# Input slabs of the mixer, and two down projections, as seven products of halves; pieces of the modulation moved

## What is computed

```python
def _swiglu(h, w1, w3, w2):
    return (jax.nn.silu(h @ w1) * (h @ w3)) @ w2

for l in range(2):                                   # D_MODEL 1024, D_FF 2816, IN_W 3584
    ml = _modulation(c, w_ada[l], b_ada[l])          # silu(c) @ w_ada + b, nine vectors of 1024
    mc = _modulation(c_ctx[None], w_ada[l], b_ada[l])
    lat = lat + 0.5 * ml[2] * _swiglu(_modulate(lat, g1, ml[0], ml[1]), *ffn1)
    cx = cx + 0.5 * mc[2] * _swiglu(_modulate(cx, g1, mc[0], mc[1]), *ffn1)
    # mixer: z = h @ w_in, cut into u, v, q, f_fw, f_bw, i, og; q, f and i drive a gated scan
    ...                                              # cx and lat += m[5] * mixer(...)
    lat = lat + 0.5 * ml[8] * _swiglu(_modulate(lat, g3, ml[6], ml[7]), *ffn2)
    ...                                              # the same for cx, in layer 0 alone
```

## Time and profile before

| | |
|---|---|
| median of 3 runs | 3027.91 us (3026.37 to 3031.58) |
| the profiled execution | 3027.08 us, of which the span is 3024.9 us |
| TensorE matmul busy | 2844.2 us, 94% of the span |
| VectorE, ScalarE, GpSimd busy | 1049.0, 555.6, 439.4 us |
| first block, from the trace | to about 2213 us |
| experts at the end | from about 2587 us, waiting for weights |

### The profile page before, as it was taken

The page is one execution under the profiler, slowest core; times in us unless marked ns, Lnnn a source line. Parts: engine busy times, 40 slices in busy tenths (PEclk is TensorE's granted clock), DMA queues, the critical chain, the costliest instruction groups (busy, mean ns, idle before and its releaser), DMA issues.

```text
span 3024.9 us, 39799 instructions
## 1 busy us (share of the span) xinstructions
PE 2844.2 (94%) x17362; PEld 2418.2 (80%) x17362; DVE 1049.0 (35%) x1988; ACT 555.6 (18%) x842; POOL 439.4 (15%) x424
## 2 busy tenths in 40 slices
PE   8999999999999998999999999999999999866666
PEld 6888888888888898889888888889988888533432
DVE  3764034431433348433013433523146412210111
ACT  2101222123211101010023206210012340200000
POOL 0000011200121177058001210028100000000000
PEclk9999999999999999999999999999999999988878
DMA  9775443344333565554544344364433228899998
GB/s 405 272 272 183 151 152 125 127 152 153 139 138 127 195 251 211 186 230 167 168 153 153 134 139 157 129 224 168 167 125 134 103 94 337 367 429 431 429 431 373
DMA packets 74144, 641.47 MB, mean 212 GB/s; under 512 B 8304, under 2 KB 9584, under 8 KB 21232
## 3 DMA queue, kind: packets, MB, share of 16 engines
q1 hardware_dynamic: 71376, 631.55, 55.1%
q10 hardware_dynamic: 2592, 7.33, 0.6%
HBM read 637.80 MB, written 1.05 MB: 211 GB/s over the span
## 4 chain that ended last, share of the span: by engine, by line
PE 82%; DMA 12%; DVE 3%; issue 1%; ACT 1%; POOL 0%; SPq 0%; DVEq 0%; ACTq 0%; POOLq 0%
PE ps L1254 29%; PE ps L1276 18%; DMA ring<-in_w_moe 12%; PE ps L1234 10%; PE ps L1451 7%; PE ps L1264 3%; PE ps L1287 3%; PE ps L1481 2%; PE ps L1055 2%; PE ps L1340 1%; DVE work L1919 1%; DVE work L1913 1%; PE ps L1458 1%; PE ps L1077 1%; DMA ring<-in_w_ada 1%
## 5 line engine op out<-in xcount | busy, mean ns | idle before, releaser
L1254 PE MATMUL ps<-ring 128*128 128x256 f32 x2560 | 560.7, 380 | 0.2 <-ACT ring L1668 0.2
L1254 PEld LDWEIGHTS ps<-ring 128*128 128x128 f32 x2560 | 485.1, 190 | 68.4 <-issue 2.0
L1276 PE MATMUL ps<-work,ring 128*128 128x256 f32 x2464 | 537.9, 379 | 2.0 <-DVE work L1913 2.0
L1276 PEld LDWEIGHTS ps<-work,ring 128*128 128x128 f32 x2464 | 466.1, 190 | 66.5 <-DVE work L1913 2.2
L1254 PE MATMUL ps<-h,ring 128*128 128x256 f32 x1600 | 350.9, 380 | 6.4 <-ACT h L1668 4.2
L1913 DVE TENSOR_TENSOR work<-work,ps 128x128 f32<-128x128 f32 (+3 forms) x414 | 151.2, 400 | 577.0 <-PE ps L1254 292.8
L1254 PEld LDWEIGHTS ps<-h,ring 128*128 128x128 f32 x1600 | 301.0, 190 | 51.7 <-issue 5.6
L2604 POOL TENSOR_TENSOR ring<-ring 128x512 f32<-128x512 f32 x174 | 240.7, 1412 | 367.2 <-DMA ring<-in_w 320.0
L2632 POOL TENSOR_TENSOR work<-work 128x128 f32<-128x128 f32 x168 | 100.2, 635 | 1193.9 <-ACT work L1694 1193.9
L1234 PE MATMUL ps<-work,ring 128*128 128x128 f32 x1856 | 218.0, 276 | 0.5 <-POOL work L2604 0.5
L1234 PEld LDWEIGHTS ps<-work,ring 128*128 128x128 f32 x1856 | 213.2, 193 | 0.7 <-POOL work L2604 0.7
(11 more groups left out here) (301 smaller groups left out, 2598.0 us busy)
## 6 DMA issues: line engine op xcount, KB each, us to landing
ring<-in_w SPq DMA_DIRECT2D x182, 1024.0 KB, 4.8
work<-in_w_moe SPq DMA_DIRECT2D x22, 4096.0 KB, 33.8
ring<-in_w_moe SPq DMA_DIRECT2D x22, 4096.0 KB, 33.3
ring<-in_w_in SPq DMA_DIRECT2D x80, 1024.0 KB, 4.8
ring<-in_w SPq DMA_DIRECT2D x56, 896.0 KB, 4.6
work<-in_w_ada SPq DMA_DIRECT2D x40, 1024.0 KB, 6.8
ring<-in_w_ada SPq DMA_DIRECT2D x32, 1024.0 KB, 4.9
ring<-in_w_out SPq DMA_DIRECT2D x16, 1024.0 KB, 4.8
```

The costliest lines, as they stand in the source:

```text
L1254: last = nc.tensor.matmul(ps[:, b, c * L:c * L + L], w[:, k * L + c * P:k * L + c * P + P], hs[cols][:, k, :], start=(k == 0), stop=(k == ...
L1276: last = nc.tensor.matmul(ps[:, b, c * L:c * L + L], w[:, k * L + c * P:k * L + c * P + P], hid[:, k0 + k, :], start=(k0 + k == 0 and c == 0),
```

## The change

Three things change.

1. The `z` slabs become halved slabs: all 14 for context and latent in layer 0, and eight for the latent in layer 1. For six of the kinds (`copied_z`: both forget gates, and i) VectorE's last additions write the final place; for the others ScalarE applies its function to the sums, an instruction more behind the five additions.
2. The `down` slabs of (1,0,0) and (1,0,1) become halved: pieces of 8, 8 and 6 blocks add into the same two banks, and the five additions come once, after the third piece. The combinations of the hidden activations are four operations on VectorE after each pair (`halve_hid`). All down results, dense ones too, are now cut 8, 8, 6 in place of 8, 7, 7.
3. Each `vada` stage is split in two halves, and the twelve pieces of layer 1 (vectors 2, 3, 4) move from the gate and up slabs of (0,0,1) to its dense down slabs.

```diff
-DOWN_K = (8, 7, 7)
+DOWN_K = (8, 8, 6)
...
+HALVED_Z = {(0, 1): range(0, 14), (0, 0): range(0, 14), (1, 0): (0, 1, 2, 3, 8, 9, 6, 7)}
+HALVED_DOWN = [(1, 0, 0), (1, 0, 1)]
...
+def copied_z(stage):
+
+    return stage[3] in (0, 1, 2, 3, 6, 7)
...
-    out = [[("vada", l, i)] for i in range(4 * first, 4 * last)] + [[], [], []]
+    out = [[("vada", l, i, c)] for i in range(4 * first, 4 * last) for c in range(2)] + [[] for _ in range(5)]
...
     run = (0, 0, 1)
-    side = [[("turn", 1, 0)]] + [[stage] for stage in more[5:]] + [[("turn", 1, 1)]] + vector_ada(1, 2, 5)
+    side = [[("turn", 1, 0)]] + [[stage] for stage in more[5:]] + [[("turn", 1, 1)]] + [[] for _ in range(8)]
     side[11] += [("sum", 1, "h"), ("norm", 1, 1, 0)]
-    plan += spread_out(gate_up(run, range(11)) + down(run, range(4)), side, 33)
+    plan += spread_out(gate_up(run, range(11)), side) + spread_out(down(run, range(4)), vector_ada(1, 2, 5))
...
+        z_halves = [shaped(ex7[:, 2 * i:2 * i + 2, :].rearrange("p a b -> p (a b)"), 4, P) for i in range(4)]
+        hid_sums = [shaped(work[:, lf_at + i * KF // 2 * P:lf_at + (i + 1) * KF // 2 * P], KF // 2, P) for i in range(4)]
...
-                        product(bx, 2, b11, a11)
+                        product(bx, 2, b11, a11, piece == 0)
                         product(bx, 0, b21, a12)
-                        pe.wait_ge(halves_done, at.halves_at[stage[1:4]] + 1)
-                        product(bx, 1, b22, s4).then_inc(x_mm, 1)
+                        if kind != "down":
+                            pe.wait_ge(halves_done, at.halves_at[run] + 1)
+                        last = product(bx, 1, b22, s4)
+                        if sums_follow(stage):
+                            last.then_inc(x_mm, 1)
...
+                        elif kind == "z" and not copied_z(stage):
+                            act.wait_ge(ev_d, at.sums_at[n])
+                            dst, func = z_target(stage)
...
+                            nc.scalar.activation(dst, src, func).then_inc(ev_a, 1)
...
+                def halve_hid(up):
...
+                    tt(s1, a21, a22, add).then_inc(dve_own, 1)
...
+                    tt(s3, a21, a11, sub)
...
+                    own(tt(s2, s1, a11, sub))
+                    tt(s4, a12, s2, sub).then_inc(hid_halved, 1)
```

More of the change, by code:

```diff
@@ L208, in with_halves @@
     slabs = [n for n, stage in enumerate(plan) if is_slab(stage)]
[L209 to L215, removed]
+    runs = dict.fromkeys(run_of(plan[n]) for n in slabs if is_halved(plan[n]))
+    for run in runs:
+        mine = [i for i, n in enumerate(slabs) if run_of(plan[n]) == run]
+        at = slabs[mine[0] - 4]
+        if run[0] != "down":
+            norm = ("norm", *run[1:], 1) if run[0] == "z" else ("norm", *run[:2], 2 * run[2])
+            ready = max(n for n in range(slabs[mine[0]]) if plan[n] == norm)
+            read = [n for n in range(slabs[mine[0]]) if plan[n][0] == "gmlp"]
+            at = max([at, ready + 1] + ([read[-1] + 1] if run[0] == 0 and read else []))
+            before[at].append(("halves", norm[2], run))
         for n, i in enumerate(mine):
@@ L251, in first_order @@
     side = vector_ada(0, 2, 9)
[L252 to L255, removed]
+    side[4] += [("bounds",)]
+    side[8] += [("rope",)]
+    side[12] += [("square", 0, p, "h") for p in range(4)]
+    side[16] += [("sum", 0, "h"), ("norm", 0, 0, 0)]
     plan += spread_out(gate_up(run, range(11)) + down(run, range(4)), side)
@@ L810, in quarters_of, with parts_of, weights_of, made @@
             return [[w.rearrange("p (k c n) -> p k c n", k=KD, c=2)[:, 4 * k:4 * k + 4, c, :] for c in range(2)] for k in range(2)]
+        def parts_of(w, n):
+            v = w[:, 0:2 * n * L].rearrange("p (k e c n) -> p k e c n", e=2, c=2, n=P)
+            return [[v[:, :, e, c, :] for c in range(2)] for e in range(2)]
+        def weights_of(stage, w):
+            return parts_of(w, DOWN_K[stage[5]] // 2) if stage[0] == "down" else quarters_of(w)
+        def made(*z):
+            engine, count = at.z_at[z]
+            return (ev_a if engine == "a" else ev_d), count
         def quarters_of_tokens(v):
@@ new lines, in first @@
+                        if kind == "down":
+                            k0 = sum(DOWN_K[:piece]) // 2
+                            ks = slice(k0, k0 + DOWN_K[piece] // 2)
+                            up = ("up", *stage[1:4], ks.stop - 1)
+                            pe.wait_ge(ev_d, at.up_at[up[1:]])
+                            pe.wait_ge(hid_halved, at.hid_halves[up[1:]])
+                            s1, s2, s3, s4 = (one[:, ks, :] for one in hid_sums)
+                            (a11, a12), (a21, a22) = ([hid_of[:, ks, e, t * P:t * P + P] for e in range(2)] for t in range(2))
+                        else:
+                            h_ready(KD - 1)
+                            h_seen = max(h_seen, 8 * at.h_norms[n])
+                            s1, s2, s3, s4 = z_halves if kind == "z" else halves
+                            (a11, a12), (a21, a22) = quarters_of_tokens(hs[stage[2]])
@@ new lines, in product @@
+                        def product(b, place, weight, act, first=False):
+                            many = weight.shape[1]
+                            for k in range(many):
+                                one, other = weight[:, k, :], act[:, k, :]
+                                last = nc.tensor.matmul(ps[:, b, place * P:place * P + P], *((other, one) if tokens_first else (one, other)),
+                                                        start=(k == 0 and (first or kind != "down")),
+                                                        stop=(k == many - 1 and sums_follow(stage)), skip_group_check=True)
@@ L2064, in first @@
                                ).then_inc(ev_d, 1)
+                            halve_hid(stage)
+                        elif kind == "down":
+                            l, s, j, p = stage[1:5]
+                            dve.wait_ge(mod_done, 5 * l + (2, 5)[j])
+                            dve.wait_ge(ev_d, at.sums_at[n])
+                            for c in range(2):
+                                last = stt(xs[s][:, 2 * p + c, :], sil[:, which, c * L:c * L + L],
+                                           mod[:, l, (2, 8)[j] * KD + 2 * p + c, s:s + 1], xs[s][:, 2 * p + c, :], mul, add)
+                            last.then_inc(ev_d, 1)
                     elif kind == "up":
```

255 lines of the change are left out of this document (166 added, 89 removed).

## The result

The changed kernel takes 3013.05 us (3012.80 to 3013.55 over four executions) against 3027.91 us before (3026.37 to 3031.58 over five). A fifth execution of the changed kernel took 4186.47 us in a slower state, with a granted clock of 0.65 where the others have 0.97, and is left out. The ratio is 0.9946, 95% interval 0.9934 to 0.9958: faster, by 14.9 us in the medians and 14.0 in the profiled executions (3013.05 and 3027.08 us), 13.7 of them in the span. I forecast 22.2 us gained, 3005.6. The mechanism was the one forecast; one part of the sum was mis-sized and others missed by less.

The account below looks back on a forecast made before the run. TensorE was taken to bound the kernel until the first block ends near 2213 us. Gains of 12.7 + 13.7 - 4.2 = 22.2 us from 3027.1 gave 3004.9, stated as 3005.6 by the median; range 2987 to 3019 us.

Parts of the forecast that it names:

- Part 1: Down slabs of (1,0,0) and (1,0,1): halving gains 14.2 us, less 1.5 at the first block's end, +12.7 us.
- Part 2: Run (0,0,1): moving layer-1 modulation pieces to the down slabs gains 13.7 us; splitting the 28 early pieces changes nothing.
- rival 4: Down slabs of (0,0,1): VectorE or SP's queue falls behind with the moved pieces; 3029 us, no change; chance 0.06.
- Part 3: 36 halved z slabs: 23.3 us gained, 22.4 lost to stops behind `gates`, 5.1 to the clock, -4.2 us.
- the 5.7 us: Layer 1's `gates`: time from the second Exp to the end of the second Ln, taken from the earlier trace.
- the 3.7 us: Layer 1's `gates`: VectorE's work after the first Ln, raised to 5.8 us because GpSimd overlaps it in part.
- the three long stops: TensorE's stops above 5 us behind `gates` in the z slabs; 1.7 us of lowered clock after each, 5.1 in all.
- The last step of the sum: Whole kernel: 3004.9 us from the profiled execution, raised because the median lies 0.8 above it, stated as 3005.6 us.
- rival 3: Stops as forecast, but clock stays down longer or additions recover a slab later: 3014 us middle, 3020.5 far end; chance 0.16.
- Rivals 2: z slabs: GpSimd does not slow `gates`, stops stay at 9.5 us, clock holds; 40.2 us gained, 2987.7; chance 0.24.
- Rival 5: z slabs: GpSimd's combination becomes the bound at some 8.9 us per slab; 3073 us, slower; chance 0.07.

Follow-up runs that it names:

- the experiment: The changed kernel with only the down slabs of (1,0,0) and (1,0,1) dense again: 3025.01 us, ratio to before 0.9984.
- the run with few columns: The changed kernel with GpSimd's combinations in z(0,0) and z(1,0) on 8 of 128 columns, leaving out part of the computation: 2996.04 us.
- the run with the pieces back: The changed kernel with the twelve layer-1 modulation pieces whole again among the gate and up pairs of (0,0,1): 3031.42 us, ratio to before 1.0003.

## Why the prediction was right, and where its sizes were off

**Part 1** (+12.7 forecast, +12.3 by the windows, 12.0 by the experiment) held, by its own step: 616 halved instructions for 352 dense ones. The end costs 2.8 and not 1.5 us. The pause of TensorE there grew by 1.65 us, near what was charged; the rest, 1.2 us, comes after it, where matmuls run slower: 32 of their instructions take 4.3 to 4.6 us where 3.73 is the row of an unbroken end.

**Part 2** (+13.7 forecast, +15.3 measured) held: the pairs took 145.9 us (146.2 forecast), with one wait of 0.8 us. The down slabs took 82.8 us for 83.6; the turn at the very end waited 0.7 us. VectorE and DMA kept up (63.3 us busy of 82.8, 265 GB/s), so rival 4 fell. One sentence was wrong: that splitting the 28 early pieces changes nothing. I read "TensorE is busy 253.7 of 255.3 us" as no room. But the 1.6 us that are missing were one avoidable stop, and busy time also includes matmuls at a lower clock, 1.7 us behind that stop; with them 3.5 us were there.

**Part 3** (-4.2 forecast, -14.8 measured) is the part that was mis-sized; its mechanism held, at each of the five places named. In its own terms: gain 23.3; stops in the z stages 7.9 + 8.7 + 10.2 = 26.8 us in place of 22.4; clock 73.9 - 5 x 12.52 = 11.3 in place of 5.1. The three sum to -14.8. The layer-0 stops were 16.6 us in all, as forecast (2.9 and 5.1 in each stage, where I said 3.1 and 5.2, and one of 0.8 before them in z(0,0)). The whole error in the stops is layer 1: 10.2 in place of 5.8. Step by step, forecast and measured: VectorE between the first Ln and the second Exp, 5.8 and 7.6 us (1554.31 to 1561.90); from the second Exp to the end of the second Ln, 5.7 and 9.7 us (1561.94 to 1571.68); VectorE's last operation, 2.4 and 1.23 us. The largest miss is thus a term that was not stretched at all: the 5.7 us came undisturbed from the earlier trace rows, but inside them ScalarE waits for four of VectorE's small operations, which took 5.2 us in place of 1.15. The other is that I stretched the 3.7 us by 1.6 after the earlier trace rows, where large operations slow by 1.8, and the small ones do worse: four of 1.14 us took 4.13. What GpSimd added on this path is 3.0 + 0.9 + 4.1 = 8.0 us, just what the stop lost in the run with few columns (10.20 to 2.23 us). And I charged the clock only behind the three long stops, 1.7 us each; all five pay, short ones too, 11.3 us in all.

The rows show what the small operations do: beside GpSimd each takes 1.03 to 1.3 us, about as long as one of GpSimd's instructions, and not its own 0.29 us; the twelve took 12.46 us in all. Single rows at the start of that stretch:

```profile
1554.31 1.23 DVE L2035 SCALAR_TENSOR_TENSOR work<-work 128x1024 f32<-128x1024 f32 x1 [0.88 <-ACT work L1796]
1554.41 2.25 POOL L2760 TENSOR_TENSOR ring<-ring 128x512 f32<-128x512 f32 x1
1555.57 1.24 DVE L2032 TENSOR_SCALAR work<-work,lb 128x256 f32<-128x256 f32 x1
```

VectorE began first and kept its 1.23 us, and GpSimd's instruction, which takes about 1.24, needed 2.25; then GpSimd held on until 1556.66 and the operation of 0.29 us took 1.24. In these rows they take turns by whole instructions, and many short ones pay once each. The Trainium skill, "SBUF — State Buffer", section "Who interferes with whom", says that VectorE and GpSimd arbitrate for one pair of ports by an exclusive lock held for the whole instruction, that the later one blocks, and that `tensor_scalar` can use the pair as well as operations with two SBUF inputs. The trace agrees, in the three rows above. I had weighed only the bare statement that there is contention, in the Trainium skill, "GPSIMD Engine Reference", section 1. By the rule of the exclusive lock each small operation can cost one instruction of GpSimd's more, an estimate of 12 x 1.24 = 14.9 us at worst, where the trace shows 9.0 (12.46 - 3.46).

**The sum and the rivals.** The total came out closer than Part 3 did, by luck: of its miss of 10.6 us, 3.5 and 1.6 us were made good by the first feed-forward and by Part 2, which gave more than forecast. (The last step of the sum is off by 0.1: 3004.9 and 0.8 make 3005.7.) The result lies near the 3014 that rival 3 named as its middle, but that rival held the stops to be as forecast, and they were 4.4 us longer. Rivals 2 and 3 mark the ends: no GpSimd effect (refuted by the run with few columns), and a clock that stays down longer (half true: all five stops pay, 1.7 to 3.1 us each). Rival 5, GpSimd as the bound, fell: between `gates` the slabs come every 6.26 us.

What stays open: the 2.7 us lost between the stages and in the second block, which the forecast put at nothing and of which one slab at 8.86 in place of 7.17 us is part; and the two ring waits in the run with the pieces back.

## What to carry to other kernels

Halving a slab shortens TensorE's work but also the time that its banks cover. Before doing it, list what stands ahead of the bank-freeing instruction in each in-order queue, and leave as many slabs dense after a long stage as its length asks for: 26 of 36 slabs halved gave 31 us more than all 36. When GpSimd gets work beside VectorE, count VectorE's instructions on SBUF there, not only their time, in every term of the path. And a stop of TensorE of 2.9 us or more cost its length plus 1.7 to 3.1 us of lowered clock here, which idle matmuls in the stop give back if they are counted right.

## What the runs showed of the hardware

- VectorE beside GpSimd, by kind: 128x256 `TENSOR_SCALAR` 1.03 us for 0.29 (mean of four); 128x1024 two-input operations 2.17 and 1.96 us for 1.23; a 128x1024 copy 1.65 for 0.69. GpSimd's three instructions took 4.7 to 4.9 us for 3.73. Operations reading PSUM kept their 1.47 us for five.
- Stops of 2.9 us were followed by a granted clock of 0.88 and 0.81 over the next 15 us, one of 10.2 us by 0.83: between these the length of the stop hardly mattered. In the run with few columns stops of 1.90 and 2.23 us were both followed by 0.88 over 14.4 us, one of 0.92 us by 1.00.
- With TensorE kept busy to within 0.4 to 0.8 us of the stop's end, the clock read 1.00.
